# The inverse of a gated delta rule: half of each level's products replaced by 32x32 block transposes on the DVE

## The reference, cut to what matters

```python
lower = jnp.where(tri_strict, jnp.einsum('bhncd,bhnsd->bhncs', k_beta, k) * decay, 0.0)
rhs = jnp.concatenate([v_beta, k_beta * jnp.exp(gc)[..., None]], axis=-1)
sol = lax.linalg.triangular_solve(eye + lower, rhs, left_side=True, lower=True,
                                  unit_diagonal=True)
...
def step(state, inp):
    qk_n, q_dec_n, k_dec_n, u_n, w_n, gl_n = inp
    v_new = u_n - jnp.einsum('bhcd,bhdv->bhcv', w_n, state)
    o_n = (jnp.einsum('bhcd,bhdv->bhcv', q_dec_n, state)
           + jnp.einsum('bhcs,bhsv->bhcv', qk_n, v_new))
    state = state * gl_n[..., None, None] + jnp.einsum('bhcd,bhcv->bhdv', k_dec_n, v_new)
    return state, o_n
```

## Time and profile before

| | |
|---|---|
| median of 3 runs | 2485.92 us (2484.38 to 2486.22) |
| profiled execution, its own time | 2485.54 us |
| its span in the trace | 2483.8 us |
| PE busy | 2440.4 us, 98% of the span |
| DVE busy | 1468.2 us, 59% |
| ACT busy | 1210.0 us, 49% |
| POOL busy | 84.5 us, 3% |
| layer A's four groups | about 1449 to 1946 us of the span |

### The profile page before, as it was taken

One profiled execution on the slowest core, in us unless ns is written; L12 is line 12 of the kernel. 1 busy time (PEld: TensorE's weight loads), 2 busy tenths in 40 slices (PEclk: granted clock), 3 DMA queues, 4 the chain that ended last, 5 costly groups with the idle time before them and its releaser, 6 DMA issues.

```text
span 2483.8 us, 36860 instructions
## 1 busy us (share of the span) xinstructions
PE 2440.4 (98%) x13228; PEld 2022.9 (81%) x13228; DVE 1468.2 (59%) x1953; ACT 1210.0 (49%) x1842; POOL 84.5 (3%) x107
## 2 busy tenths in 40 slices
PE   8999999999999999999999999999999899999999
PEld 6788888888888888888888778787878788888887
DVE  5656554556566654566655666667565555655654
ACT  5444544444556543445544554545463445555543
POOL 0002100000200000000000010100000000000000
PEclk9999999999999999999999999999999999999999
DMA  7756555555765655565466444535353375555545
GB/s 252 234 184 172 163 171 202 189 192 181 221 190 173 194 189 195 184 194 180 150 208 195 142 137 121 146 104 153 110 147 108 128 225 183 164 172 174 180 167 169
DMA packets 286896, 431.33 MB, mean 174 GB/s; under 512 B 32560, under 2 KB 126000, under 8 KB 286640
## 3 DMA queue, kind: packets, MB, share of 16 engines
q1 hardware_dynamic: 280960, 421.12, 54.5%
q10 hardware_dynamic: 5808, 8.41, 1.0%
HBM read 427.37 MB, written 7.08 MB: 175 GB/s over the span
## 4 chain that ended last, share of the span: by engine, by line
PE 93%; DVE 2%; DMA 2%; ACT 1%; issue 1%; DVEq 1%; SPq 0%; ACTq 0%
PE gemm L491 28%; PE gemm L493 27%; PE gemm L492 27%; PE aux L1676 2%; DMA raw<-in_w_in 1%; DVE w_lo L470 1%; PE aux L1939 1%; PE aux L1952 1%; PE aux L1949 1%; ACT w_hi L460 1%; PE aux L1837 1%; PE aux L1909 1%; PE aux L1772 1%; PE aux L2130 0%; PE aux L1891 0%
## 5 line engine op out<-in xcount | busy, mean ns | idle before, releaser
L470 DVE TENSOR_TENSOR w_lo<-raw,w_hi 128x1024 fp32r<-128x1024 f32 (+1 forms) x800 | 966.1, 1219 | 580.7 <-ACT w_hi L460 570.2
L460 ACT ACTIVATE w_hi<-raw 128x1024 fp32r<-128x1024 f32 (+1 forms) x800 | 822.1, 1042 | 590.7 <-PE gemm L493 498.8
L491 PE MATMUL gemm<-w_lo,hT_hi 128*128 128x512 f32 (+1 forms) x2304 | 913.5, 397 | 5.9 <-DVE w_lo L470 3.6
L493 PE MATMUL gemm<-w_hi,hT_lo 128*128 128x512 f32 (+1 forms) x2304 | 896.0, 389 | 0.0
L492 PE MATMUL gemm<-w_hi,hT_hi 128*128 128x512 f32 (+1 forms) x2304 | 894.8, 388 | 0.0
L491 PEld LDWEIGHTS gemm<-w_lo,hT_hi 128*128 128x128 f32 x2304 | 433.5, 188 | 98.3 <-issue 9.1
L493 PEld LDWEIGHTS gemm<-w_hi,hT_lo 128*128 128x128 f32 x2304 | 433.0, 188 | 91.2
L492 PEld LDWEIGHTS gemm<-w_hi,hT_hi 128*128 128x128 f32 x2304 | 433.9, 188 | 83.5
L491 PE MATMUL gemm<-w_lo,yT_hi 128*128 128x512 f32 x472 | 184.4, 391 | 1.2 <-DVE w_lo L470 1.2
L493 PE MATMUL gemm<-w_hi,yT_lo 128*128 128x512 f32 x472 | 183.7, 389 | 0.0
L492 PE MATMUL gemm<-w_hi,yT_hi 128*128 128x512 f32 x472 | 183.7, 389 | 0.0
(11 more groups left out here) (292 smaller groups left out, 1956.6 us busy)
## 6 DMA issues: line engine op xcount, KB each, us to landing
raw<-in_w_up SPq DMA_DIRECT2D x336, 256.0 KB, 3.2
raw<-in_w_in SPq DMA_DIRECT2D x144, 512.0 KB, 4.5
raw<-in_a_w_in SPq DMA_DIRECT2D x128, 512.0 KB, 3.6
raw<-in_b_w_in SPq DMA_DIRECT2D x128, 512.0 KB, 4.1
raw<-in_w_down SPq DMA_DIRECT2D x76, 512.0 KB, 4.6
raw<-in_w_branch SPq DMA_DIRECT2D x32, 512.0 KB, 4.7
raw<-in_w_out SPq DMA_DIRECT2D x32, 512.0 KB, 4.3
raw<-in_a_w_out SPq DMA_DIRECT2D x32, 512.0 KB, 3.6
```

What stands on the lines that cost most here:

```text
L460: nc.scalar.activation(hi, src, ACT.Copy).then_inc(S("hi_done"), 1)
L470: nc.vector.tensor_tensor(lo, src, hi.bitcast(F32), ALU.subtract).then_inc(S("lo_done"), 1)
L491: nc.tensor.matmul(dst, xh, wl[:, k, :], start=h["start"] and k == 0, stop=False)
L493: mm = nc.tensor.matmul(dst, xl, wh[:, k, :], start=False, stop=h["stop"] and k == h["n"] - 1)
```

## The change

- **T by transposes.** T of levels 0 to 4 is block diagonal with blocks of at most 32. DVE makes it from U by one instruction that transposes 32x32 blocks: at level 0 from SBUF, at levels 1 to 4 from bank 3, ahead of the copy of U'. The 16 products against the identity, the 16 products of T' in levels 1 to 4 and ACT's five copies in these levels go. Level 5 stays.
- **One slot fewer.** Z of level 1 follows the second gram product in step 4; all later steps of `delta` come one slot earlier. The multiplication by `dec` that makes `qk` moves behind W1 of level 1.
- **Gate sums ahead.** The two instructions that fill `dec` with gates move from step 1 to the end of `factors`, ahead of DVE's read of the last k tile.
- **Scan.** PE waits for `zdec` alone before the second scan product; `tmp` has a semaphore of its own (`d_z`), awaited after it. Scan products 2 to 5 go to bank 3, output products to bank 2.
- **Order on DVE.** In a slot, DVE does the step of the group ahead of that of the side, in both layers, since `stack` is shared. PE and ACT keep theirs.
- ACT drains once between the sums of squares of a part's two blocks, and POOL makes `ATl` of level 1 as soon as A is there.

```diff
@@ POOL delta
-                            pool.wait_ge(S("d_U1"), gi + 1)
+                            pool.wait_ge(S("d_gram_out"), gi * 2 + 1)
@@ ACT delta
-                act.wait_ge(S("d_T1"), gi + 1)
-                A(Tm[:, :, :], AX[2][:, :].rearrange("p (a c) -> p a c", c=C), ACT.Copy).then_inc(S("d_T"), 1)
...
-                    if l < LEVELS - 1:
-                        A(Tm[:, :, :], AX[2][:, :].rearrange("p (a c) -> p a c", c=C), ACT.Copy).then_inc(S("d_T"), 1)
@@ DVE factors
                 V.tensor_tensor(fac[:, 4, :, :], fac[:, 2, :, :], edec[:, :, hs], ALU.mult)
                 dve.drain()
+                dve.wait_ge(S("chunk_masks"), 1)
+                for tb in range(TB):
+                    e = V.tensor_tensor(dec[:, tb * HG:(tb + 1) * HG, :], rep(m_le[:, :], HG), each(gg[:, tb, hs], P), ALU.mult)
+                e.then_inc(S("d_gm"), 1)
@@ DVE delta
-                                       op0=ALU.mult, op1=ALU.add).then_inc(S("d_U1"), 1)
+                                       op0=ALU.mult, op1=ALU.add)
+                dve.drain()
+                V.transpose(Tm[:, :, :].rearrange("p a c -> p (a c)"), Um[:, :, :].rearrange("p a c -> p (a c)")).then_inc(S("d_T"), 1)
...
                     dve.wait_ge(S("d_TU"), n)
                     if l < LEVELS - 1:
+                        V.transpose(Tm[:, :, :].rearrange("p a c -> p (a c)"), AX[3][:, :]).then_inc(S("d_T"), 1)
                         V.tensor_copy(Um[:, :, :], AX[3][:, :].rearrange("p (a c) -> p a c", c=C)).then_inc(S("d_U"), 1)
...
-                                each(fac[:, 4, 0, :], HD), ALU.mult)
-                V.tensor_copy(tmp[:, 0, :], AX[2][:, :]).then_inc(S("d_scan_out"), 1)
+                                each(fac[:, 4, 0, :], HD), ALU.mult).then_inc(S("d_scan_out"), 1)
+                V.tensor_copy(tmp[:, 0, :], AX[2][:, :]).then_inc(S("d_z"), 1)
@@ DVE stack
-                        run(half, 8, side(i + 1, part - 1) if part else side(i, 2), g)
+                        run(half, 8, g, side(i + 1, part - 1) if part else side(i, 2))
@@ PE delta
-                for tb, a, h, rows_, c in chunks():
-                    m = MM(AX[2][rows_, c * C:(c + 1) * C], Um[rows_, c, :], idc[rows_, :], start=True, stop=True)
-                m.then_inc(S("d_T1"), 1)
                 gram(xc)
-                yield
...
-                        for a in range(2 if l < LEVELS - 1 else 1):
+                        for a in range(0 if l < LEVELS - 1 else 1):
                             rows_ = slice(a * C, (a + 1) * C)
                             MM(AX[2][rows_, c * C:(c + 1) * C], Um[rows_, c, :], W1[rows_, c, :], start=True, stop=True)
...
-                    m = MM(AX[2][:, c], ks[:, c], zdec[:, c], start=True, stop=True)
+                    m = MM(AX[3][:, c], ks[:, c], zdec[:, c], start=True, stop=True)
                 m.then_inc(S("d_scan"), 1)
+                pe.wait_ge(S("d_z"), gi + 1)
```

More of the change, by code:

```diff
@@ L862, in delta @@
                 e.then_inc(S("d_exp"), 1)
+                for _ in range(12):
+                    yield
+                act.wait_ge(S("d_TU"), gi * (LEVELS - 1) + LEVELS - 1)
+                A(Tm[0:C, :, :], AX[2][0:C, :].rearrange("p (a c) -> p a c", c=C), ACT.Copy).then_inc(S("d_T"), 1)
                 yield
-                yield
-                yield
-                act.wait_ge(S("d_T1"), gi + 1)
-                A(Tm[:, :, :], AX[2][:, :].rearrange("p (a c) -> p a c", c=C), ACT.Copy).then_inc(S("d_T"), 1)
[L868 to L871, removed]
-                    if l < LEVELS - 1:
-                        A(Tm[:, :, :], AX[2][:, :].rearrange("p (a c) -> p a c", c=C), ACT.Copy).then_inc(S("d_T"), 1)
-                    else:
-                        A(Tm[0:C, :, :], AX[2][0:C, :].rearrange("p (a c) -> p a c", c=C), ACT.Copy).then_inc(S("d_T"), 1)
-                    yield
                 act.wait_ge(S("d_corner"), gi * 2 + 1)
@@ L884, in delta @@
                 act.wait_ge(S("d_scan_o"), gi * 2 + 1)
-                A(o_rows[:, 0, :], AX[3][:, :], ACT.Copy).then_inc(S("d_scan_o_out"), 1)
+                A(o_rows[:, 0, :], AX[2][:, :], ACT.Copy).then_inc(S("d_scan_o_out"), 1)
                 yield
@@ L889, in delta @@
                     c = slice(h * HD, (h + 1) * HD)
-                    e = A(o_rows[:, 1, c], AX[3][:, c], ACT.Copy, scale=egc[:, 1, bass.ds(gi * HG + h, 1)])
+                    e = A(o_rows[:, 1, c], AX[2][:, c], ACT.Copy, scale=egc[:, 1, bass.ds(gi * HG + h, 1)])
                 e.then_inc(S("d_scan_o_out"), 1)
@@ L1390, in delta @@
             def delta(gi):
[L1391 to L1395, removed]
                 yield
@@ L1429, in delta @@
                                            in1=rep(idc[:, :], TB * HG), op0=ALU.mult, op1=ALU.add).then_inc(S("d_W1"), 1)
+                    if l == 1:
+                        dve.wait_ge(S("d_gram"), gi * 2 + 2)
+                        for tb in range(TB):
+                            b = slice(tb * HG, (tb + 1) * HG)
+                            e = V.tensor_tensor(qk[:, b, :], AX[tb][:, :].rearrange("p (a c) -> p a c", c=P), dec[:, b, :], ALU.mult)
+                        e.then_inc(S("d_gram_out"), 1)
                     yield
@@ L1457, in delta @@
                 dve.wait_ge(S("d_scan"), gi * 5 + 4)
-                V.tensor_copy(tmp[:, 1, :], AX[2][:, :]).then_inc(S("d_scan_out"), 1)
+                V.tensor_copy(tmp[:, 1, :], AX[3][:, :]).then_inc(S("d_scan_out"), 1)
                 yield
@@ L1461, in delta @@
                 dve.wait_ge(S("d_scan"), gi * 5 + 5)
-                V.tensor_tensor(o_rows[:, 1, :], o_rows[:, 1, :], AX[2][:, :], ALU.add).then_inc(S("d_scan_out"), 1)
+                V.tensor_tensor(o_rows[:, 1, :], o_rows[:, 1, :], AX[3][:, :], ALU.add).then_inc(S("d_scan_out"), 1)
                 yield
@@ L1518, in stack @@
                 run(half, 5, g)
-                run(half, 3, s, g)
-                run(half, single, s, g)
-                run(half, 12 - single, s, g, g)
+                run(half, 3, g, s)
+                run(half, single, g, s)
+                run(half, 12 - single, g, g, s)
                 finish(g)
@@ L1988, in delta @@
                 for h, c in enumerate(heads):
-                    m = MM(AX[2][:, c], kS[:, h, :], St[:, c], start=True, stop=True)
+                    m = MM(AX[3][:, c], kS[:, h, :], St[:, c], start=True, stop=True)
                 m.then_inc(S("d_scan"), 1)
@@ L1992, in delta @@
                 for h, c in enumerate(heads):
-                    m = MM(AX[3][:, c], qS[:, h, :], St[:, c], start=True, stop=True)
+                    m = MM(AX[2][:, c], qS[:, h, :], St[:, c], start=True, stop=True)
                 m.then_inc(S("d_scan_o"), 1)
@@ L1997, in delta @@
                 for h, c in enumerate(heads):
-                    m = MM(AX[2][:, c], Uf[:, HG + h, :], vs[:, 1, c], start=True, stop=True)
+                    m = MM(AX[3][:, c], Uf[:, HG + h, :], vs[:, 1, c], start=True, stop=True)
                 m.then_inc(S("d_scan"), 1)
@@ L2002, in delta @@
                 for h, c in enumerate(heads):
-                    m = MM(AX[2][:, c], qk[:, HG + h, :], tmp[:, 1, c], start=True, stop=True)
+                    m = MM(AX[3][:, c], qk[:, HG + h, :], tmp[:, 1, c], start=True, stop=True)
                 m.then_inc(S("d_scan"), 1)
```

19 lines of the change are left out of this document (5 added, 14 removed).

## The result

| | before | after |
|---|---|---|
| median of 4 runs each on one chip | 2485.99 us (2484.38 to 2486.22) | 2442.44 us (2441.83 to 2443.01) |
| profiled execution, its own time | 2485.54 us | 2443.01 us |
| its span | 2483.8 us | 2440.7 us |

The ratio is 0.9826, 95% interval 0.9814 to 0.9838. The change saves 43.5 us by the medians and 42.5 us by the profiled executions. I had forecast 34.4 us, and my range ended at 2445: the sign and most terms were right, but the gain was larger than any sum I had allowed.

The account below looks back on a forecast made before the run. PE, busy 98% of the span, was taken as the bound. Terms of 36.8 us less 2.4 gave 34.4 us off 2485.54: 2451 us, own range 2446 to 2457, widened to 2445 to 2463 to leave at most 2 in 10 out.

Parts of the forecast that it names:

- The products: Levels 1 to 4 on PE: 16 products less are worth 0.93 us, 16 times, 14.9 us saved.
- level 0: On PE, the 16 products against the identity go: 1.08 us, four times, 4.3 us saved.
- The transpose: On DVE: taken as 0.7 us, by the copy of the same tile; at most 1.4 us.
- The waits for the gate sums, for `zdec` and at W1: PE's waits at group start, before scan 2 and at W1 of level 3 go: 5.6, 5.2 and 1.0 us.
- the waits of 0.8 (`z_rows`) and 0.7 us (ACT's copy): Group 3, two steps in a slot: 0.8 stays between scan 4 and 5, 0.7 from corner 2 to scan 1.
- End of group 3: Waits where steps share a slot gain 0.3 us, the `zT_lo` wait 2.8 us, the clock 1.0 us.
- `o_rows` wait: End of group 3, between scan 5 and the turn of `o_rows`: the wait of 3.04 us stays.
- POOL in the way: `w_lo` on DVE meets POOL's mask product, T of level 5 late: 0.8 us in three turns, 2.4 us given back.
- Z of level 1: Sharing a slot with the gram product saves a switch between small and large products; counted at nothing.
- the rivals: DVE late more often, 2462 us (0.17); only PE's work, 2466 (0.07); small products, 2461 (0.04); slower than before (0.02).
- the clock term: End of group 3: without the second pause the low-clock stretch shortens, 1.0 us taken from 0 to 2.6.
- the collision: `w_lo` on DVE under POOL's mask product ahead of level 5: 2.4 us lost, range 0 to 3.0.

Follow-up runs that it names:

- e2: Kernel before with only the block transposes, in place of the T products and ScalarE's copies of levels 0 to 3: 2467.82 us, ratio 0.9929.
- e9: Kernel after with Z of level 1 and all later steps one slot later again on PE, ACT and DVE: 2449.88 us, ratio 0.9862.
- e3: Kernel before with only the gate sums' operand formed ahead of the group, at the end of the side stage: 2474.72 us, ratio 0.996.
- e6: Kernel after with a 128x128 copy on DVE ahead of the `w_lo` that met POOL's mask product, in three loop turns: 2445.76 us, ratio 0.984.
- e7: Kernel after with a 128x128 copy on DVE behind the `w_lo` that met POOL's mask product: 2446.43 us, ratio 0.9845.
- e1: Kernel after with DVE's scaling of y one step later in the loop, so the tok read stands ahead of it: 2442.35 us, ratio 0.9829.
- e5: Kernel after with y's scaling one step later and PE's loop of layer A written out three times: 2439.04 us, ratio 0.9812.
- e10: Kernel after with only PE's loop of layer A written out: 2441.80 us, ratio 0.9829.
- e4: Kernel before with only DVE's order changed, the group's work ahead of the side stage's in each step: 2477.72 us, ratio 0.997.

## Why the prediction was right, and where it fell short

**Right.** The products: without T' a half with TU lasts 4.02 us instead of 4.96, the 0.93 us that I counted 16 times; level 0 went for 1.08 us each; `e2` measured 16.8 us where its items came to 19. The transpose costs 0.71 us for 0.7. The waits for the gate sums, for `zdec` and at W1 went, with the 0.23 us in group 3 as their only heir, a wait outside level 5 where I had said that there would be none. In group 3 the waits of 0.8 (`z_rows`) and 0.7 us (ACT's copy) came as 0.78 and 0.68. Layer B shows no wait of PE.

**Wrong, as a range.** The profiled executions differ by 42.5 us, 8.1 more than the forecast. By steps, the largest first:

- *End of group 3.* I took 1.0 us for the clock out of a span of 0 to 2.6, and said that the `o_rows` wait "stays". The half behind the wait for `zT_lo` gave 5.29 - 2.85 = 2.4 us, the turn 0.9, the wait 3.04 - 2.21 = 0.8: 3.1 us beyond the 1.0. `e9` shows that the first and the last of these hang on the slot; the 0.9 doesn't, since the turning is as fast in `e3` and `e9`, with both pauses in place. The `o_rows` wait fell because the order around it changed: DVE's `w_lo` of 1.2 us stood between the mean and the reciprocal (at 1936.93) and now stands ahead of the mean (at 1896.29), so that the scaling starts 6.6 and not 7.4 us after the last scan product. The profiled execution had the best case, no low clock at all; three other kernels with the same end lost 1.3 us there. This is the term that was sized worst; I chose near the middle of 0 to 2.6 where the rows gave two states, slow and not slow.
- *POOL in the way.* I took 2.4 us back for it. The step that failed is "Under it for 1.2 us it should lose 1.0": I had both starting within 0.1 us, and let DVE lose. It won three times of three. `e6` shows that the price was right once POOL starts first: each turn is 0.9 to 1.1 us longer (124.05, 123.93 and 123.87), of which the copy itself is at most 0.2, for 0.8 forecast. Which of the two would start first, 0.1 us apart, my sum could not tell; in the trace after, POOL's record even starts 0.01 us ahead, and still POOL was held. And I had read one direction only, though the kernel before shows the other at level 1 of every group (its rows stand with `e7`).
- *A removed wait is worth more than its row.* The wait is counted from the modelled end of the last matmul (0.39 us after its start), and the next one would have started 0.23 us after it: 0.16 us more for each of 13 waits, 2.0 us.
- *Z of level 1* behind the gram product saved a switch, which I "counted at nothing": about 0.2 us four times, 0.8 us.
- *The wait for tok* was missed: 3 x 1.27 = -3.8 us. I moved `delta` one slot up and its steps ahead of the side, but did not look at what then stood ahead of the tok read at the end of slot 24.
- *The pauses at the wrap*, +2.5 us, were not forecast either. `e1`, `e5` and `e10` show that they are the jump of PE's loop, and that they and the waits for tok nearly cancel.
- 1.2 us lie ahead of layer A, in stages that the change doesn't touch (1387.50 against 1386.27 at the same matmul): the difference of two executions.

The sum is 3.1 + 2.4 + 2.0 + 0.8 - 3.8 + 2.5 + 1.2 = 8.2 us, against 8.1. Of the rivals none came: the clock term and the collision were among the largest errors, and both lay on the good side, where I had left only 0.02. The wait for tok and the pauses at the wrap, two misses of 3.8 and 2.5 us, nearly cancel in the sum by luck. The upper end of my range, by its own terms (+1.0, +0.6, +4 and +1.5), is 2458 and not 2457, which changes nothing.

**Open.** Why PE asked for the loop's first instructions in time in the kernel after, and so late in `e1` that it stood for 1.4 us, with the same program on PE, isn't settled. The packet came 117.2 us after the group's masks product in the kernel after and 117.6 to 117.7 in `e1`, hardly moved by the wait of 1.11 us that only the first has. Yet in `e6` and `e7`, whose earlier waits make the turn about 1 us longer, it came after 118.2 to 118.5 us. So it follows some of PE's waits and not this one; no run separated that. The slot's gain in `e9` adds up: 5.2 us of the stretch and 2.4 us of the slow half, less the 0.2 us that the three turns of the loop take less there, are the 7.4 us between the medians; that it is 8.8 us against the kernel before is within what the chips differ by. Which of the two pauses at the end of group 3 the clock hangs on, and why it was low in three of eight kernels behind the one that is left, stays open. The version `e5` is the fastest, 3.4 us below the change; their intervals overlap, but its turn is 1.4 us shorter in each of three.

## What to carry to other kernels

Where a stretch holds two pauses close together, price the clock as two states and not as a mean: removing one gave its 2.8 us and, in five of eight profiled executions, 2.4 us of slow matmuls as well; in the other three it gave 1.1 us of them. Where two engines exclude each other, work out who starts first to within 0.1 us, and what the loser holds up, before taking a loss. A wait that goes can uncover one that it had hidden, a loop's jump as well as another engine; test such a pair together, since each edit alone measured nothing.

## What the runs showed of the hardware that I had not expected

- The jump at the end of PE's loop cost 0.85 to 1.41 us a turn in the kernel before and in `e1` to `e4` and `e9`, PE going on 2.66 to 2.80 us after an instruction packet; with the packet 2.9 to 3.0 us ahead of need there was no pause, but for the one of 0.37 us in `e7`. The trace puts it down to another engine. Writing out PE's loop took the pause away.
- DVE and POOL exclude each other in both directions: 1.30 became 2.37 us on POOL, 1.21 became 2.31 us and 0.21 became 1.31 us on DVE. W1, which reads PSUM, kept its 0.68 us while POOL's product ran.
- A 128x512 fp32 transpose in 32x32 blocks takes 0.71 us on DVE, about the 0.69 us of a copy.
